# Two products of 256 moving columns in place of one of 512, in an FP32 transformer kernel

## The reference

```python
# first block: differential attention and a sparse attention, then SwiGLU
h = rms_norm(x, attn_pre_norm)
mix = hybrid_mixer(h, ...)                       # h @ w_in, attentions, @ w_out
x = x + rms_norm(mix, attn_post_norm)
h = rms_norm(x, ffn_pre_norm)
f = (silu(h @ w_gate) * (h @ w_up)) @ w_down     # 1024 -> 2816 -> 1024
x = x + rms_norm(f, ffn_post_norm)
# second block, two layers: short convolution with forgetting attention, then SwiGLU;
# a conformer convolution (31 taps, LayerNorm), then SwiGLU
```

## Time and profile before

| | |
|---|---|
| time, median of 3 runs | 1901.34 us (1896.58 to 1903.04) |
| the profiled execution: its own time | 1899.32 us |
| its span, first to last instruction | 1897.1 us |
| granted TensorE clock, mean over the span | 0.991 |
| TensorE matmul busy | 1861.5 us, 98%, 9410 products |
| TensorE weight load busy | 1510.6 us, 80%, 9410 loads |
| GpSimd busy | 1239.9 us, 65% |
| VectorE busy | 811.3 us, 43% |
| ScalarE busy | 430.2 us, 23% |

### The profile page before, as it was taken

One profiled execution on the slowest core, in us unless ns is written; L12 is line 12 of the kernel. 1 busy time (PEld: TensorE's weight loads), 2 busy tenths in 40 slices (PEclk: granted clock), 3 DMA queues, 4 the chain that ended last, 5 costly groups with the idle time before them and its releaser, 6 DMA issues.

```text
span 1897.1 us, 25590 instructions
## 1 busy us (share of the span) xinstructions
PE 1861.5 (98%) x9410; PEld 1510.6 (80%) x9410; DVE 811.3 (43%) x1365; ACT 430.2 (23%) x880; POOL 1239.9 (65%) x743
## 2 busy tenths in 40 slices
PE   9999999999999999999999999999999999999997
PEld 7886678888888898777888888889778888888886
DVE  6355755433331144254543333015984453334103
ACT  4336663111110021131311111003334221111000
POOL 7975537866666657664876667557665686666652
PEclk9999999999999999999999999999999999999998
DMA  6431002333333214212233333222323233323311
GB/s 208 132 114 46 12 1 78 110 90 93 95 113 107 79 45 158 83 49 67 89 100 100 88 101 116 100 71 67 100 67 90 78 100 89 99 89 110 106 61 45
DMA packets 44877, 168.27 MB, mean 89 GB/s; under 512 B 4984, under 2 KB 7288, under 8 KB 44672
## 3 DMA queue, kind: packets, MB, share of 16 engines
q1 hardware_dynamic: 44496, 164.56, 27.9%
q10 hardware_dynamic: 304, 2.64, 0.4%
HBM read 165.07 MB, written 2.11 MB: 88 GB/s over the span
## 4 chain that ended last, share of the span: by engine, by line
PE 91%; DVE 4%; POOL 3%; issue 1%; ACT 1%; DMA 0%; POOLq 0%; SPq 0%; DVEq 0%
PE psum L583 27%; PE psum L585 27%; PE psum L584 27%; PE psum L801 2%; POOL w_lo L470 1%; PE psum L785 1%; DVE h_lo L1556 1%; DVE tmp L1598 1%; PE psum L827 1%; POOL w_hi L467 1%; PE psum L633 1%; PE psum L824 1%; PE psum L917 1%; PE psum L931 1%; POOL x L491 1%
## 5 line engine op out<-in xcount | busy, mean ns | idle before, releaser
L470 POOL TENSOR_TENSOR w_lo<-raw,w_hi 128x1024 fp32r<-128x1024 f32 (+1 forms) x286 | 748.4, 2617 | 23.8
L583 PE MATMUL psum<-h_hi,w_hi 128*128 128x512 f32 (+1 forms) x1744 | 663.8, 381 | 13.4 <-POOL w_lo L470 7.4
L584 PE MATMUL psum<-h_lo,w_hi 128*128 128x512 f32 (+1 forms) x1744 | 657.0, 377 | 0.0
L585 PE MATMUL psum<-h_hi,w_lo 128*128 128x512 f32 (+1 forms) x1744 | 657.0, 377 | 0.0
L467 POOL TENSOR_SCALAR w_hi<-raw 128x1024 fp32r<-128x1024 f32 (+1 forms) x286 | 323.7, 1132 | 472.5 <-PE psum L585 446.6
L583 PEld LDWEIGHTS psum<-h_hi,w_hi 128*128 128x128 f32 x1744 | 327.6, 188 | 90.3 <-issue 15.9
L585 PEld LDWEIGHTS psum<-h_hi,w_lo 128*128 128x128 f32 x1744 | 327.2, 188 | 67.7
L584 PEld LDWEIGHTS psum<-h_lo,w_hi 128*128 128x128 f32 x1744 | 327.3, 188 | 66.1 <-issue 0.2
L583 PE MATMUL psum<-g_hi,w_hi 128*128 128x512 f32 (+1 forms) x594 | 219.1, 369 | 0.0
L584 PE MATMUL psum<-g_lo,w_hi 128*128 128x512 f32 (+1 forms) x594 | 218.5, 368 | 0.0
L585 PE MATMUL psum<-g_hi,w_lo 128*128 128x512 f32 (+1 forms) x594 | 218.5, 368 | 0.0
(11 more groups left out here) (282 smaller groups left out, 1876.4 us busy)
## 6 DMA issues: line engine op xcount, KB each, us to landing
raw<-in_wide SPq DMA_DIRECT2D x239, 512.0 KB, 3.6
raw<-in_down SPq DMA_DIRECT2D x48, 704.0 KB, 4.0
decay<-decay_rows ACTq DMA_DIRECT2D x1, 2048.0 KB, 7.8
out<-x SPq DMA_DIRECT2D x16, 128.0 KB, 1.7
x<-in_xt SPq DMA_DIRECT2D x3, 512.0 KB, 6.9
x<-in_xt ACTq DMA_DIRECT2D x1, 512.0 KB, 4.6
angles<-in_angles SPq DMA_DIRECT2D x1, 512.0 KB, 10.4
cols<-in_cols SPq DMA_DIRECT2D x1, 221.0 KB, 4.4
```

The lines of the kernel that those rows point to most:

```text
L470: nc.gpsimd.tensor_tensor(w_lo[:, slot, 0:w], raw[:, j % RAW, 0:w], w_hi[:, slot, 0:w].bitcast(F32), ALU.subtract).then_inc(units_split, 1)
L583: pe.matmul(out_ap, lhs[0], rhs[0], start=first, stop=False)
L584: pe.matmul(out_ap, lhs[0], rhs[1], start=False, stop=False)
L585: return pe.matmul(out_ap, lhs[1], rhs[0], start=False, stop=last)
```

## The change

`three` looks at its output. Where that is not 512 columns wide, it does as before. Where it is, it goes through the left and then the right 256 columns, and issues the three products for each: six products, six weight loads, with the stationary order high, high, low, high, high, low. The flag `start` is set on the first product of the left half alone. The callers, the waits and the semaphore counts stay.

```diff
             def three(out_ap, lhs, rhs, first, last):
 
-                pe.matmul(out_ap, lhs[0], rhs[0], start=first, stop=False)
-                pe.matmul(out_ap, lhs[0], rhs[1], start=False, stop=False)
-                return pe.matmul(out_ap, lhs[1], rhs[0], start=False, stop=last)
+                if out_ap.shape[-1] != S:
+                    pe.matmul(out_ap, lhs[0], rhs[0], start=first, stop=False)
+                    pe.matmul(out_ap, lhs[0], rhs[1], start=False, stop=False)
+                    return pe.matmul(out_ap, lhs[1], rhs[0], start=False, stop=last)
+                for half in (slice(0, H), slice(H, S)):
+                    out, moving = out_ap[:, half], [part[:, half] for part in rhs]
+                    pe.matmul(out, lhs[0], moving[0], start=first and half.start == 0, stop=False, skip_group_check=True)
+                    pe.matmul(out, lhs[0], moving[1], start=False, stop=False, skip_group_check=True)
+                    mm = pe.matmul(out, lhs[1], moving[0], start=False, stop=last, skip_group_check=True)
+                return mm
```

## The result

The changed kernel was timed in 20 runs beside 20 of the one before. The medians over all runs are 1897.18 us after and 1899.84 us before. The ratio given for the comparison is 0.9949, 95% interval 0.9932 to 0.9965; it sorts out runs that lie over 1.5% above the fastest as disturbed, and here that sorting also drops undisturbed ones of the changed kernel, so the medians over all runs are the plainer measure. The forecast was 1865.6 us.

What follows compares the result with a forecast made beforehand. TensorE, holding 91% of the chain, was taken as the bound. The terms 40.8 + 0.3 - 0.4 - 4.0 - 1.0 gave 35.7 us gained, a median of 1865.6 us; range 1857 to 1918.

Steps and rivals of the forecast that it cites:

- What bounds the kernel, the counts, the cost of 512 columns: TensorE holds 91% of the chain; 6402 products become two each, 9410 to 15812; one of 512 columns costs 233.3 ns.
- What 256 columns cost: 256-column products start 113.3 or 118 ns apart: each old product gains 6.7 ns or loses 2.7.
- the 1915 it states: Rival, all activation products slow: median 1919.7 us, or 1915 if 118.2 ns is rounded up from 117.8; chance 0.18.
- The load as a floor: All split products: a weight load takes 112 ns, so a pair costs at least 224 ns, gaining at most 9.3.
- Which rhythm I take: Long streams run at 113.3 ns, as in the last down output; activation products gain 40.8 us; chance 0.55.
- Rival 2: Each stage settles on its own, half of the old products in each rhythm: 11 us gained, 1890; chance 0.15.
- The term for what lies outside the SwiGLU parts: Outside: activation products gain 6.67 ns each, weights 0.3 us; lost: fox_parts 0.4, slow short streams 4.0, conformer 1.0 us.
- The conformer: From 1390.98 to 1425.01 us GpSimd's sums and splits hold the chain, so TensorE waits there; 1.0 us given back.
- The work said to hide things: In the loop GpSimd (3.8 us per unit of 5.44) and the DMA (0.33) keep up; 1.6 us of cover left.
- Rival 3: Gate and up loop outgrows instruction memory, each of 27 repeats refetches: 46 to 97 us more, 1911 to 1963; chance 0.05.
- Rival 4: The 20 ns above column time come with any width; a pair costs what one did: 1899 to 1903; chance 0.07.
- the formula: N / 2.4 + 2.5 ns per product: a pair pays 2.5 ns twice, 16 us more, about 1917.

Runs made afterwards that it cites:

- the 25 times above: Changed kernel, its runs less one far outside, plus six of an unaltered repeat: 1870.2 to 1912.1 us, in four groups.
- the execution of 1870.97 us: The profiled execution of the changed kernel, fastest of its 20, against the kernel before: 1870.97 us with a span of 1868.7.

## Why the prediction was wrong, step by step

**What bounds the kernel, the counts, the cost of 512 columns:** right. TensorE holds the chain before and after, 15812 products ran, and the 1920 products of the loop in 218 us are what 0.680 us for six gives.

**What 256 columns cost:** right in both rhythms, 113.3 and 117.7 ns; I rounded the slow one up to 118, so its loss for an old product is 2.3 ns and not 2.7. Three slow streams came to 1908.7 to 1912.1 us, not 1919.7. (With 117.8 ns the forecast's own figures give 1901.3 + 15.7 = 1917 us, not the 1915 it states.) The load as a floor was right for the mean, 110 to 112 ns with 128 columns against 112.

**Which rhythm I take: this step failed.** I wrote that the operand and the order do not fix the rhythm and that a stream takes one after an interruption and keeps it; both were shown for the split streams with `h` and `g`. Then I chose one rhythm for all long streams, from the likeness of the order in the earlier trace rows. The experiments with other orders show that this likeness counts for nothing. I had also miscounted the openings: the trace before has five, four with records of 281 ns and one with 276. Their code is the same after the change, and there the first and third are fast and the fifth slow, the other way round than before. Each long stream gets its rhythm anew in each execution: of 75 SwiGLU streams in the 25 times above, by their groups, 9 + 22 + 6 = 37 were slow and 38 fast. Even odds for three streams put the middle at one or two of three in the slow rhythm, 1884 to 1897 us. Rival 2, the mixture, named the right thing at 1890 us; I gave it 0.15 since I read one execution's rhythms as properties of places.

**The term for what lies outside the SwiGLU parts:** mis-sized. The sum had (6126 - 4266) x 6.67 = 12.4 us, plus 0.3, less 0.4, 4.0 and 1.0, so 7.3 us. The split outside alone gave 1.0003 of the time before. The profiles say it too. From a loop's first product to the first column sum behind the down outputs, each SwiGLU part took 343.1 us before and 333.7 in the execution of 1870.97 us; three times 9.48 is 28.4 us, the whole difference of the spans, and all that lies outside took the same time. Waits took little (TensorE's for `w_lo` are 8.1 us against 7.5, all of its idle time 37.8 against 35.6); most of the gain was never there: outside, the products of the new split (L589 to L591) stand 116.0 ns apart on the mean (4124 distances within streams), a pair costs 232.0 ns, and the old products outside cost 232.6 (2020 distances), not 233.3. Over 2136 products that is 1.3 us. Some of these streams are slow in both profiled executions, and the products with `op` and `fox_parts` moving stand at 119 to 120 ns. The conformer shows that I had the wait wrong there. Its stretch, after the change:

```profile
1303.00:1429.00 126.00, 124.96 (x1060) 123.84 (x1059) 99.52 (x143) 44.35 (x71) 88.82 (x55) 1.00 0.31 93
```

That is 1060 products in the 126 us that held 532 before, twice as many less four, with TensorE as busy as before: no gain, and no new wait for GpSimd either (TensorE waits for it 0.2 us there before and not at all after): the pairs cost what the old products cost. The fastest execution fits the rest: 4266 x 6.67 = 28.5 us, and 1899.3 - 28.5 = 1870.8 against 1870.97 us.

**The work said to hide things:** right. GpSimd kept up with units of 5.44 us (152.08 us busy in the 218 of a loop), and no wait was added in the loops. Rival 3, instruction fetch, did not come up; between 366 and 560 us, nearly all of rounds two to ten of the first loop, no DMA packet carries instructions, so a round of an estimated 1.7 packets stays.

**Rival 4 and the formula.** In the long streams a pair does not cost what one product did. By the formula that the Trainium skill (TensorE: Matmul & The Clock Gate, section "Back-to-back issue gap") gives, a pair would cost 2.5 ns more than one product; the runs show 6.7 ns less or 2.3 ns more. By it one product of 512 columns takes 215.8 ns; 233.3 were measured. The section gives the formula for an isolated product and says itself that it does not fit a stream of loads and products, which the prediction left out.

What stays open is what the state is. The runs show a state of the stream, kept by 256-column products, set to slow by one product of 512, set to fast by at most three pairs of them, swapped by three and kept by six. Records of 276 and 281 ns go with it, and in the slow rhythm one load in three of 192 ns. That points to the way loads and products fall against each other in time, but why it happens, and why one, two, three and six whole products act as they do, no run shows.

## What to carry to other kernels

A split that makes the products about as short as their weight loads is worth 3% of the time of the long streams here, but only if the stream is steered: unsteered it gained 0.1% at the median and anything from a gain of 1.5% to a loss of 0.6% in single runs; two whole products at the head of a unit made it 1.4 to 1.5% at the median. Where the split gains nothing, as outside the SwiGLU parts here, it can be left out. Where a trace shows two spacings for one shape, consider that they may be outcomes that change from execution to execution, as here, and count how many long streams draw one. Read the distribution of single times before the median: here steps of equal size pointed to a few independent two-way outcomes, and their size gave the length of the streams.

## What the runs showed that was not expected

- The same program runs the same 2941 products in 333.3 or 346.4 us, from execution to execution, with TensorE at a granted clock of 1.00 in both.
- A single product of 512 columns among 256-column ones decides over the cost of the following ones: with one per unit nearly all units of the SwiGLU parts were slow (1913.7 us), with two nearly all fast (1872.5), with three they alternated (1891.9).
- In a slow stream one weight load in three has a record of 192 ns, in a fast one none: all have 187 or 188.
- Products with 128 and 384 columns cost 0.86 us for three pairs, against 0.68 for halves, with the same columns and loads.
